# mLSTM scores from the convolved input through an on-chip Wq Wk^T, gate products of two tiles in four column groups, and one selection matrix

## The reference

```python
xm, z = jnp.split(u @ w_up, 2, axis=-1)            # 2048 channels each
xc = jax.nn.silu(conv_centred(xm, conv_w, conv_b)) # three taps
q = blockdiag(xc, w_q)                             # 4x4 blocks
k = blockdiag(xc, w_k)
v = blockdiag(xm, w_v)
gates = jnp.concatenate([q, k, v], axis=-1) @ w_gate + b_gate   # 16 per token
s = jnp.einsum('bhjd,bhsd->bhjs', q, k * DH ** -0.5) * decays   # 4 heads of 512 channels
h = (h_normed + skip * xc) * jax.nn.silu(z)
```

## Time and profile before

| What | Value |
|---|---|
| runs | 2116.59, 2119.5, 2119.77 us; median 2119.5 us |
| profiled execution | 2115.98 us, of it 2114.3 us span |
| mean granted TensorE clock | 0.979 |
| TensorE busy (PE) | 2035.9 us, 96% of the span |
| VectorE, ScalarE busy | 1217.2 us, 652.3 us |
| chain that ended last, by engine | PE 89%, DVE 7%, ACT 2%, DMA 1% |

### The profile page before, as it was taken

One profiled execution on the slowest core, in us unless ns is written; L12 is line 12 of the kernel. 1 busy time (PEld: TensorE's weight loads), 2 busy tenths in 40 slices (PEclk: granted clock), 3 DMA queues, 4 the chain that ended last, 5 costly groups with the idle time before them and its releaser, 6 DMA issues.

```text
span 2114.3 us, 25270 instructions
## 1 busy us (share of the span) xinstructions
PE 2035.9 (96%) x9698; PEld 1603.7 (76%) x9698; DVE 1217.2 (58%) x1640; ACT 652.3 (31%) x665; POOL 85.8 (4%) x157
## 2 busy tenths in 40 slices
PE   7799999999999999999999999999999998799999
PEld 3368888886876676888888688888867667398998
DVE  3467667548556747776754967232373235765445
ACT  3342222233232123222222322222253344434343
POOL 0000000000000000000000000000000001000000
PEclk8699999999999999999999999999999998899999
DMA  8225555432230023555544255222312123034553
GB/s 299 100 100 199 197 187 191 150 128 80 93 108 18 0 72 120 189 197 182 189 156 139 101 194 193 88 100 99 129 60 75 55 79 111 20 120 159 179 181 118
DMA packets 48321, 272.55 MB, mean 129 GB/s; under 512 B 5380, under 2 KB 6020, under 8 KB 24840
## 3 DMA queue, kind: packets, MB, share of 16 engines
q1 hardware_dynamic: 28536, 195.21, 26.0%
q0 software_dynamic: 19728, 76.55, 10.7%
HBM read 270.69 MB, written 1.05 MB: 129 GB/s over the span
## 4 chain that ended last, share of the span: by engine, by line
PE 89%; DVE 7%; ACT 2%; DMA 1%; issue 1%; POOL 0%; DVEq 0%; ACTq 0%; SPq 0%
PE ps L1265 24%; PE ps L1266 24%; PE ps L1267 24%; PE ps L1533 3%; PE ps L1543 2%; PE ps L1258 2%; DVE tn L797 1%; PE ps L1605 1%; DVE act_lo L783 1%; PE ps L1459 1%; PE ps L1688 1%; DVE w_lo L709 1%; PE ps L1444 1%; DMA ada_raw<-ada_stream_dram 1%; PE ps L1591 1%
## 5 line engine op out<-in xcount | busy, mean ns | idle before, releaser
L1265 PE MATMUL ps<-act_hi,w_hi 128*128 128x512 f32 (+1 forms) x2728 | 988.5, 362 | 18.7 <-DVE w_lo L709 9.9
L1266 PE MATMUL ps<-act_lo,w_hi 128*128 128x512 f32 (+1 forms) x2728 | 981.5, 360 | 0.0
L1267 PE MATMUL ps<-act_hi,w_lo 128*128 128x512 f32 (+1 forms) x2728 | 981.2, 360 | 0.0
L709 DVE TENSOR_TENSOR w_lo<-w_raw,w_hi 128x2048 fp32r<-128x2048 f32 x172 | 394.0, 2291 | 494.5 <-ACT w_hi L384 494.5
L1265 PEld LDWEIGHTS ps<-act_hi,w_hi 128*128 128x128 f32 x2728 | 517.9, 190 | 113.8 <-DVE act_lo L783 13.8
L1267 PEld LDWEIGHTS ps<-act_hi,w_lo 128*128 128x128 f32 x2728 | 517.9, 190 | 76.2
L1266 PEld LDWEIGHTS ps<-act_lo,w_hi 128*128 128x128 f32 x2728 | 518.0, 190 | 75.5 <-issue 1.0
L384 ACT ACTIVATE w_hi<-w_raw 128x2048 fp32r<-128x2048 f32 x172 | 329.0, 1913 | 626.2 <-PE ps L1267 626.2
L731 DVE SCALAR_TENSOR_TENSOR ada_w<-ada_w,cond_bc 128x1024 f32<-128x1024 f32 x128 | 156.1, 1219 | 0.0
L731 DVE SCALAR_TENSOR_TENSOR ada_prod<-ada_w,cond_bc 128x1024 f32<-128x1024 f32 x128 | 156.0, 1219 | 0.0
L427 ACT ACTIVATE silu_g<-ps 128x1024 f32<-128x1024 f32 (+1 forms) x44 | 40.5, 920 | 307.3 <-PE ps L1267 307.3
(11 more groups left out here) (197 smaller groups left out, 1139.8 us busy)
## 6 DMA issues: line engine op xcount, KB each, us to landing
w_raw<-w_stream_dram SPq DMA_DIRECT2D x172, 1024.0 KB, 4.8
ada_w<-ada_rows_dram POOLq DMA_DIRECT2D x128, 512.0 KB, 3.7
ada_raw<-ada_stream_dram POOLq DMA_DIRECT2D x8, 1024.0 KB, 8.9
bd<-bd_dram SPq DMA_DIRECT2D x4, 768.0 KB, 6.1
edecay<-log_decay_dram SPq DMA_DIRECT2D x4, 512.0 KB, 19.1
h<-tokens_dram SPq DMA_DIRECT2D x1, 2048.0 KB, 17.0
wg<-wg_dram SPq DMA_DIRECT2D x3, 512.0 KB, 5.4
w3aug<-w3aug_dram SPq DMA_DIRECT2D x4, 260.0 KB
```

Source lines behind the costliest of these rows:

```text
L709: dve.tensor_tensor(w_lo[:, g % 2, :], w_raw[:, g % 2, :], w_hi[:, g % 2, :].bitcast(F32), ALU.subtract).then_inc(w_lo_done, 1)
L1265: pe.matmul(out, wh, xh, start=start, stop=False)
L1266: pe.matmul(out, wh, xl, start=False, stop=False)
L1267: return pe.matmul(out, wl, xh, start=False, stop=stop)
```

## The change

The query matrices are loaded transposed, and for each head four matmuls (`head_matrix`) multiply the transposed query and key matrices of its four tiles into the combined one; ScalarE copies the result over the query slot of `bd`. q_head is then made with the combined matrix, and the scores take the SiLU output itself, kept for a head in `xc_head`, in the place of `k_head`. The k product and its copy are gone. `qkv(j)` does both tiles' q in two banks, the values of tile 0, the four gate products of both tiles in column groups 0, 32, 64 and 96, and the values of tile 1. The gate sums lie in four groups of 16 partitions; VectorE copies two and ScalarE two into a zeroed `gsum`, and four matmuls against one selection matrix of 128 rows (`gate_sel`) add them. `w_comb` moves to another place in SBUF. The waits on `qkv_done` are now on `v_done`, and the convolution waits on `xc_ready` only.

```diff
@@ ScalarE, mLSTM input stage
                     if j > 0:
-                        act.wait_ge(qkv_done, tile - 1)
+                        act.wait_ge(v_done, 2 * j)
                     act.activation(pad[:, t, :, 1:257], ...).then_inc(xm_ready, 1)
+                if j % 2 == 0:
+                    act.wait_ge(m_done, j // 2 + 1)
+                    act.activation(bd[:, j // 2 % 2, :, 0, :], ps[:, 6, :].rearrange("p (a c) -> p a c", a=HT),
+                                   ACT.Copy).then_inc(m_evac, 1)
                 split_w(G_MLUP + j + 2)
                 for t in range(2):
-                    act.wait_ge(xc_step, 3 * (2 * j + t) + 3)
-                    act.activation(xc[:, t, :], xc[:, t, :], ACT.Silu).then_inc(xc_ready, 1)
+                    tile = 2 * j + t
+                    act.wait_ge(xc_step, 3 * tile + 3)
+                    if tile >= HT:
+                        act.wait_ge(xs_done, tile - HT + 1)
+                    act.activation(xc_head[:, tile % HT, :], xc[:, t, :], ACT.Silu).then_inc(xc_ready, 1)
                 for t in range(2):
                     tile = 2 * j + t
-                    act.wait_ge(kq_done, tile + 1)
-                    act.activation(q_head[:, tile % HT, :], ps[:, 5, 0:LAT], ACT.Copy)
-                    act.activation(k_head[:, tile % HT, :], ps[:, 4, :], ACT.Copy).then_inc(kq_evac, 1)
+                    act.wait_ge(q_done, tile + 1)
+                    act.activation(q_head[:, tile % HT, :], ps[:, 4 + t, 0:LAT], ACT.Copy).then_inc(q_evac, 1)
+                for t in range(2):
+                    tile = 2 * j + t
                     act.wait_ge(v_done, tile + 1)
                     act.activation(v_tok[:, :, tile * P:tile * P + P], ...).then_inc(v_evac, 1)
                 if j == 7:
                     split_w(G_MLUP + 10)
+                    act.wait_ge(v_done, IT)
+                    act.wait_ge(pad_zero, 3)
+                    for g in (2, 3):
+                        act.activation(gsum[32 * g:32 * g + 16, :], ps[32 * g:32 * g + 16, 7, :],
+                                       ACT.Copy).then_inc(gates_out, 1)
@@ VectorE
             dve.memset(pad[:], 0.0).then_inc(pad_zero, 1)
+            dve.memset(gsum[:], 0.0).then_inc(pad_zero, 1)
...
                     if j > 0:
-                        dve.wait_ge(qkv_done, tile - 1)
-                        dve.wait_ge(xs_done, tile - 1)
+                        dve.wait_ge(xc_ready, tile - 1)
...
-            dve.wait_ge(sel_done, 2)
+            dve.wait_ge(sel_done, 1)
@@ TensorE
+            def head_matrix(hd):
+                pe.wait_ge(bd_loaded[hd % 2], 16 * (hd // 2 + 1))
+                if hd > 0:
+                    pe.wait_ge(v_evac, HT * hd)
+                for k in range(HT):
+                    b = bd[:, hd % 2, k]
+                    mm = pe.matmul(ps[:, 6, k * P:k * P + P], b[:, 0], b[:, 1], start=True, stop=True)
+                mm.then_inc(m_done, 1)
+            def values(j, t):
+                tile = 2 * j + t
+                pe.wait_ge(v_evac, tile)
+                for s in range(4):
+                    n0 = 1 + (s % 2) * P
+                    mm = pe.matmul(ps[:, 6, s * P:s * P + P], pad[:, t, s // 2, n0:n0 + P],
+                                   bd[:, tile // HT % 2, tile % HT, 2], start=True, stop=True)
+                mm.then_inc(v_done, 1)
             def qkv(j):
+                hd = j // 2
+                if j % 2 == 0:
+                    pe.wait_ge(m_evac, hd + 1)
+                    if hd > 0:
+                        pe.wait_ge(sc_evac, hd)
                 for t in range(2):
                     tile = 2 * j + t
...
-                    pe.matmul(ps[:, 5, 0:LAT], b[:, 0], xc[:, t, LATC], start=True, stop=True)
-                    pe.matmul(ps[:, 4, :], b[:, 1], xc[:, t, :], start=True, stop=True).then_inc(kq_done, 1)
...
-                    pe.matmul(ps[0:16, 7, :], w_comb[:, tile, 0, :], xc[:, t, :], ...)
-                    pe.matmul(ps[32:48, 7, :], w_comb[:, tile, 1, :], pad[:, t, :, 1:257], ...)
+                    pe.wait_ge(xc_ready, tile + 1)
+                    if tile >= 2:
+                        pe.wait_ge(q_evac, tile - 1)
+                    pe.matmul(ps[:, 4 + t, 0:LAT], bd[:, hd % 2, tile % HT, 0], xc_head[:, tile % HT, LATC],
+                              start=True, stop=True).then_inc(q_done, 1)
+                values(j, 0)
+                for t in range(2):
+                    tile = 2 * j + t
+                    for kind, x in enumerate((xc_head[:, tile % HT, :], pad[:, t, :, 1:257])):
+                        g = 64 * t + 32 * kind
+                        pe.matmul(ps[g:g + 16, 7, :], w_comb[:, tile, kind, :], x, start=j == 0, stop=j == 7,
+                                  skip_group_check=True)
+                values(j, 1)
             up(0)
             for j in range(8):
+                if j % 2 == 0:
+                    head_matrix(j // 2)
                 up(j + 1)
                 qkv(j)
...
-            for g in range(2):
-                if g == 1:
-                    pe.wait_ge(sel_done, 1)
-                for r in range(4):
-                    a = slice(32 * g, 32 * g + 16)
-                    mm = pe.matmul(ps[R, 4 + r, :], ident[a, 32 * g + 4 * r:32 * g + 4 * r + 4], gsum[a, :],
-                                   start=g == 0, stop=g == 1)
-                mm.then_inc(sel_done, 1)
+            for r in range(4):
+                mm = pe.matmul(ps[R, 4 + r, :], col("gate_sel", 4 * r, 4), gsum[:], start=True, stop=True)
+            mm.then_inc(sel_done, 1)
```

More of the change, by code:

```diff
@@ L67, in column_places @@
                     ("b_gate", 4), ("mean_w", 1), ("eps_norm", 1), ("eps_ml", 1), ("eps_filt", 1),
-                    ("neg_t", 2), ("tap_mask", 2), ("one", 1), ("cond_sel", 2), ("warm", 1)):
+                    ("neg_t", 2), ("tap_mask", 2), ("one", 1), ("cond_sel", 2), ("gate_sel", 16), ("warm", 1)):
         at[name] = n
@@ L166, in build @@
         xs = over("xs", [P, IT, LAT], scr_at + 16384)
-        k_head = over("k_head", [P, HT, TOK], scr_at + 32768)
+        xc_head = over("xc_head", [P, HT, TOK], scr_at + 32768)
         q_head = over("q_head", [P, HT, LAT], scr_at + 40960)
@@ L181, in build @@
         pd = [over("pd0", [P, 2, TOK], act_at + 4096), over("pd1", [P, 2, TOK], ada_at + 4096)]
+        w_comb = over("w_comb", [P, IT, 2, 16], tmp_at + 4160)
         score_b = over("score_b", [P, HEADS, 2, LAT], tmp_at)
@@ L322, in _ @@
                 load_w(g)
-            sp.wait_ge(qkv_done, 4)
+            sp.wait_ge(v_done, 4)
             sp.dma_start(bd[:, 0], dram["bd"][2]).then_inc(bd_loaded[0], 16)
@@ L1579, in qkv @@
-                    pe.wait_ge(xc_ready, tile + 1)
-                    if tile > 0:
-                        pe.wait_ge(kq_evac, tile)
-                    pe.matmul(ps[:, 5, 0:LAT], b[:, 0], xc[:, t, LATC], start=True, stop=True)
-                    pe.matmul(ps[:, 4, :], b[:, 1], xc[:, t, :], start=True, stop=True).then_inc(kq_done, 1)
-                    if tile > 0:
-                        pe.wait_ge(v_evac, tile)
-                    for s in range(4):
-                        n0 = 1 + (s % 2) * P
-                        mm = pe.matmul(ps[:, 6, s * P:s * P + P], pad[:, t, s // 2, n0:n0 + P], b[:, 2],
-                                       start=True, stop=True)
@@ L1590, in qkv @@
-                    mm.then_inc(v_done, 1)
-                    pe.matmul(ps[0:16, 7, :], w_comb[:, tile, 0, :], xc[:, t, :], start=tile == 0, stop=tile == IT - 1,
-                              skip_group_check=True)
-                    pe.matmul(ps[32:48, 7, :], w_comb[:, tile, 1, :], pad[:, t, :, 1:257], start=tile == 0,
-                              stop=tile == IT - 1, skip_group_check=True).then_inc(qkv_done, 1)
+                    pe.wait_ge(xc_ready, tile + 1)
+                    if tile >= 2:
+                        pe.wait_ge(q_evac, tile - 1)
@@ L1601, in _ @@
                     hd = j // 2
-                    pe.wait_ge(kq_evac, HT * (hd + 1))
+                    pe.wait_ge(q_evac, HT * (hd + 1))
                     for jt in range(2):
                         for k in range(HT):
-                            mm = pe.matmul(ps[:, 4 + jt, :], q_head[:, k, jt * P:jt * P + P], k_head[:, k, :],
+                            mm = pe.matmul(ps[:, 4 + jt, :], q_head[:, k, jt * P:jt * P + P], xc_head[:, k, :],
                                            start=k == 0, stop=k == HT - 1)
@@ L1795, in lay_out @@
             vec[32 * g + cd, at["cond_sel"] + cd] = 1.0
+    for g in range(4):
+        for k in range(16):
+            vec[32 * g + k, at["gate_sel"] + k] = 1.0
     fsmall = np.zeros((P, 384), f)
@@ L1809, in diagonal @@
         return out.reshape(IT, P, P)
-    diag3 = np.stack([diagonal(w) for w in (ml_w_q, ml_w_k, ml_w_v)])
+    diag3 = np.stack([diagonal(ml_w_q).transpose(0, 2, 1), diagonal(ml_w_k).transpose(0, 2, 1), diagonal(ml_w_v)])
```

19 lines of the change are left out of this document (7 added, 12 removed).

## The result

| | before | changed |
|---|---|---|
| first comparison, median | 2118.28 us (4 runs) | 2090.39 us (4 runs, 2089.05 to 2091.54) |
| profiled execution | 2115.98 us, span 2114.3 | 2091.54 us, span 2089.9 |
| TensorE busy | 2035.9 us | 2010.5 us |
| mean granted clock | 0.979 | 0.980 |

The ratio of the first comparison is 0.9878, 95% interval 0.9866 to 0.9890. The same two kernels were compared twice more, on two chips: 2115.79 against 2090.81 (0.9883, 0.9864 to 0.9903) and 2115.22 against 2093.49 (0.9897, 0.9880 to 0.9913). So the gain is 22 to 28 us, with the middle comparison and the profiled pair at 25.0 and 24.4. The forecast was 2096, a gain of 23.6. Part of the scatter lies ahead of the changed stage: the first q product starts at 1577.39 in the profile before, at 1577.51 in this one and at 1579.34 in a later profile of the same program.

The account below looks back on a forecast made before the run. TensorE was taken to bound the input stage, and VectorE's gate-row chain the stretch from the selection to the third `z_block`. Gains of 18.6 + 6.2 − 1.2 = 23.6 us off 2119.5 gave 2096 us, range 2089 to 2102.

Parts of the forecast that it names:

- its own narrower range: Total time: the main forecast case's range, 2092 to 2099 us, chance 0.72.
- the rival in which TensorE bounds the blocks behind the selection: Behind the selection: its whole 7.45 us counts and the clock's 2.4 returns; gain 28.5, total 2091; chance 0.07.
- Pairs of tiles: Input stage: a pair falls from 6.59 to 3.90 us, 21.5 in 8 pairs; bounds 13.8 to 22.4.
- changes of kind: Within a pair: 0.11 us lost where TensorE passes between kinds of work, taken as unchanged.
- Head matrices: Input stage: 0.98 us each, 2.9 in all for heads 1 to 3; head 0's fits in TensorE's idle time.
- The copy of the first values: Inside a pair: ScalarE's copy of tile 0's v ends 0.26 us before tile 1's v needs the bank; no cost.
- the worry: Rival in the pairs: the v copy is late, 0.5 us a pair; gain 19.6, total 2100; chance 0.12.
- SiLU in front of qkv(7): Before the last pair: tile 1's SiLU ends 6.15 us into the block, wanted at 6.28; just hidden.
- The selection: After `up(9)`: gate rows begin at 4.82 us instead of 11.00, held by VectorE's `w_lo`; gain 6.18 us.
- the two regimes: TensorE sets the time up to the end of `up(9)`; from the selection to the third `z_block`, the gate-row chain does.
- The hole and the clock: Before the third `z_block`: TensorE idles 5.2 us; the slowed clock costs 1.2 us, bounds 0 to 2.2.
- The forecast's last sentence of the sum: Behind the last `z_block`: everything that follows moves as a whole.

## Why the prediction was right

The forecast of 2096 (2089 to 2102) held the result, 2090.39, near its fast end. In absolute time the forecast is 5.6 us too slow, outside its own narrower range of 2092 to 2099, and the result stands closer to the 2091 of the rival in which TensorE bounds the blocks behind the selection. The number alone would not have decided between the two; the third block's wait of 4.67 us for `w_lo` does, and it is the forecast's. Much of the distance is no term of the sum but its base: 23.6 us were taken from 2119.5, the median of three runs, and in the later comparisons the kernel before has medians of 2115.2 to 2116.7 over 13 to 15 runs. Against the middle comparison (2115.79 and 2090.81) the forecast is 5.1 us too slow, 3.7 of it by the base and 1.4 by the gain, 23.6 against 25.0. By its own steps, in the profiled pair:

- **Pairs of tiles**: forecast 3.90 us, a gain of 2.69 a pair and 21.5 in all; measured 22.4 in all. A pair takes 3.74 us when a block follows, 3.81 when the scores follow, and 3.93 in `qkv(7)`; before, each took 6.59. Most of the 0.11 us for changes of kind, carried over from the old order, is not there in the new one, and 22.4 is what the prediction gave as the bound for that. That a set of four costs what two did (0.98; forecast 0.97) was read rightly from another stage; the run with two groups shows it by taking it away.
- **Head matrices**: 0.81 each (forecast 0.98), the first in the old idle time as foretold. The stage gained 20.18 us, against 18.6: 0.9 of the difference comes from the pairs, 0.5 from here, and 0.2 from the last scores and the blocks. The 0.98 was read in front of gate products; four such matmuls take 0.92 or 0.81 in front of a block.
- **The copy of the first values**: 0.28 us to spare, forecast 0.26. The run with the gate products first shows that the worry was real: without the cover 0.96 us a pair are lost. The Trainium skill's rule on the emptying of PSUM ("TensorEngine Tiling (Array Packing)", Performance Considerations) thus costs nothing in this order (0.28 us to spare), and holds in that one (0.69 us of waiting for the copy).
- **SiLU in front of qkv(7)**: forecast just hidden, 0.13 us to spare. It was not quite: it ended 6.22 us into the block (forecast 6.15), and the weight load of the second q product has to wait for it, which the sum did not have. The cost is 0.12 us, once.
- **The selection**: the gate rows moved from 11.00 to 4.86 us (forecast 4.82), gain 6.14 (6.18). That the selection's own 7.4 us don't count in full was the point of the two regimes, and the unchanged 15.11 us shows it.
- **The hole and the clock**: 4.67 us of idle time (forecast 5.2, since the two blocks ahead of it took 11.8 us and not 11.3). Behind it the third block took 1742.61 − 1735.30 = 7.31 us, where the same piece was 6.18 before, so 1.13 lost against 1.2 taken. The clock stood at half for 3.4 us from 1735.21 on, as the block began. As "TensorE: Matmul & The Clock Gate" (the Trainium skill, HAM oscillation) has it, the burst behind the wait begins slow; the trace agrees, and the cost is half of the 2.2 us that the prediction put to that rule. In the third profile of the kernel the slow stretch was twice as long.

From the first q product to the fourth block that makes 20.18 + 6.14 − 1.13 = 25.2 us. At the first weighting of the scores it is 25.0, at the end of the span 24.5, counted likewise. The forecast's last sentence of the sum, that all behind the last block moves as a whole, is the weakest: the clock stood at half for 20.5 us in the attention stage instead of 17.1, and across the three profiles of the changed kernel this stage varies by 4 us. It is a piece of luck that the two profiles of the first comparison both missed the second fall of the clock; with it the gain from the first q product to the end is 20.3 us. The medians of the three comparisons differ (27.9, 25.0, 21.7). In the profiles single executions differ by this stage and by the time ahead of the first q product, which ranges over 4.5 us; that the same makes the difference between the medians is likely and not shown. What remains open is which of them is nearest on a given chip; all lie in the forecast range.

What the prediction did not follow out is the hole. It priced it as a price of the change, and it was time to be had: three moves of instructions in VectorE's and ScalarE's programs give some 6 us in the profile. The experiments show that the hole had three causes in a row, each hidden by the one before: w_lo of the third block, w_lo of the fourth, and ScalarE's wait for the gate rows.

## What to carry to other kernels

Where an engine is busy without a gap, a removed instruction is worth its start-to-start time; where it waits, only the part up to the next engine's readiness counts, so read the start of the *consumer*, not the end of the producer. When a gain of one stage is missing from the total, compare the stages behind it and ahead of it one by one. Independent narrow products that go to different column groups share the array, and a set of them between two products that share a PSUM bank hides the copy between those. When a hole in an engine's work is moved by reordering, look for the next wait in the same row of waits before timing it: one move alone showed nothing here, nor did two; three showed 6 us.

## What the hardware showed unexpectedly

- A selection of 3.6 us with 128 rows and 4 columns left the clock at 1.00 in the stretch behind it (1718.9 to 1724), in each profile of the new selection, while in the old one, with 16 rows and 4 columns and 10.9 us long, it fell after some 3 us. Whether rows or the shorter length made the difference was not tried.
- A second fall of the clock in the attention stage, of 6.8 us, came in one of three profiles of one program and cost 4 us (45.95 against 42.05 and 42.17); with the selection alone it came in two of two (45.67 and 45.70, against 41.75 twice in the kernel before).
- With small filler matmuls at its start, the half clock of the attention stage fell from 20.5 to 10.2 us in all, and the stage was 1.0 us longer: the second set of products met a new fall.
